# Hybrid decoder trunk on one core: where four chunks of the mixer's output are transposed, and how its early output products fill the slots of pairs 4 and 5

## The chip, the cores and the metric

One core of one Trainium2 chip runs the whole program. The time is the device time of one launch in microseconds; the median of the runs is compared. The engines are named as in the profile: PE is TensorE (products and transposes), PEld its weight loads, DVE is VectorE, ACT is ScalarE, POOL is GpSimd, SP is the engine that issues most DMAs.

## What is computed

Two layers, each a feed-forward block (SwiGLU, 2816 wide), a mixer and a second feed-forward block, every one followed by a layer norm of `alpha*x + block(x)`; 512 tokens, 1024 channels, float32. The change is within the mixer:

```
proj = x @ w_in                       # q, k, v of 6 forgetting heads, gates, q, k, v of 4 differential heads, SGU input
y_fox  = softmax(q k / 8 + c_q - c_k, causal) v            # 6 heads of 64 channels: chunks 0 to 2
a      = softmax(q1 k1) - lam * softmax(q2 k2)             # differential heads, two maps each
y_diff = rms_norm(a v) * g * (1 - lam_init)                # 4 heads of 64 channels: chunks 3 and 4
y_sgu  = u * (tril(w_s) @ layer_norm(g) + b_s)             # 6 heads of 64 channels: chunks 5 to 7
m = concat(y_fox, y_diff, y_sgu) @ w_out                   # 8 chunks of 128 channels
```

## The kernel before

Every float32 product is made from three products of split operands (high and low parts, written `hi` and `lo`): hi·hi, hi·lo, lo·hi (`product`, line 984). A split is a ScalarE copy for the high part and a VectorE or GpSimd subtraction for the low part. Weights come in tiles of 128 x 2048 in three slots, A, B and D; one tile in a slot is overwritten only when the products that read its predecessor are done.

**The head stage** (`heads`, line 1258) works on ten heads in five pairs, in the order forgetting, differential, forgetting, differential, forgetting. The code counts them 0 to 4 (`BODIES`); this text calls them pairs 1 to 5. A pair has 8 steps (`STEPS`): two heads times four blocks of 128 query rows, which attend to 128, 256, 384 and 512 keys. There are 40 steps, counted 0 to 39 (`G`); pair 4 is steps 24 to 31. In a step G, TensorE does in this order: `scores(G)`, one piece of other work ("slot 1"), `values(G - 2)`, `turn_p(G - 1)` (transposes of P), and another piece ("slot 2"). A differential head has two score maps. For each step VectorE takes the row maximum (L1872), ScalarE the exponential (L902) and the copy of the transposed P (L909, `p_out`), and VectorE divides and, for differential heads, mixes the two maps (L1887 to L1893). Each engine runs these in a fixed order, and waits on counting semaphores.

**The other work.** A generator `between` hands it out, one piece for each slot. In pairs 1 to 3 it is `project(l, b + 2)` (line 1194): the queries into PSUM bank 6, the keys into bank 7, 16 pieces of three 512-column products that read `xhi` and `xlo`, the mixer's input. The projection of pair 5 is the last reader of the input and of the projection's weight tiles in slot A. From pair 4 on it is `early(l)` (line 1233), for 32 slots in pairs 4 and 5:

- It waits for the key of pair 5 (`qk_ok`), then transposes the four chunks of `EARLY` (7, 0, 5, 6) of the mixer's output, one for each slot, into banks 6 and 7 (`turn_y`, line 1200; four transposes each). ScalarE copies them to `xhi` (`y_hi`, L916), and VectorE makes `xlo` (`y_lo`, L1833). The third and fourth turn wait for the low parts of the first and second.
- Then the early output products (`early_output`): for six of the eight output tiles the four early chunks, for the last two only two, 28 pieces. The first two chunks use the W_o tile in slot B, the other two the one in slot A. Tiles alternate between banks 6 and 7, and VectorE adds each finished one to the residual (`early_add`, L1513) at steps 28, 30, 32, 34, 36 and 38.

The W_o tile in slot A is split in halves: `query_half(5)` at step 20, `key_half(5)` at step 24 on ScalarE (L696), behind the exponentials, the copy of P and the key's eviction; GpSimd subtracts each half (L616). The second half waits until the last projection is done. `lo_ok["A"]` counts both. The remaining chunks (3, 1, 4, 2) are turned late (`LATE_TURNS`) and multiplied after the last step. `rms` does the differential norm on VectorE in pairs 3 and 5 (L1848 to L1864, `RMS_AT`). SP puts each pair's q and k to memory (L445) and refills slot A behind that; GpSimd loads them back as stacks for the scores.

The tiles `hl` (ten slots of 512 columns) and `thi` hold the split activations of the feed-forward blocks. In the head stage only slots 0 to 3 of `hl` are used, for q and k.

The lines that set the order of the early work:

```
EARLY = [(7, "B", 0), (0, "B", D), (5, "A", 0), (6, "A", D)]
...
                    next(between, None)
                    if G >= 2:
                        values(G - 2)
                    if G >= 1:
                        turn_p(G - 1)
                    next(between, None)
```

Of the kernel before, what the change touches and what calls it, by code (L numbers as in the profile page):

```python
# [5 lines left out]
ALU = mybir.AluOpType  # L6
# [80 lines left out]
EARLY_BODY = 3  # L87
WHOLE = 6
LATE_TURNS = {1: 4, 2: 5, STEPS - 1: 6}
LATE_BANK = [0, 2, 6, 7, 4, 5, 6, 7]  # L90
# [23 lines left out]
def build(nc, x_in, a_w, b_w, d_w, gb_row, gb_col, mix_row, mix_col, ws_in, lamv, out):  # L114
    ctx = ExitStack()
    with ctx:
# [215 lines left out]
        qhi, qlo, khi, klo = (hl[:, i, :] for i in range(4))  # L332
        pt = [s32[:, 1, :], s32[:, 3, :]]
        pos = res[64:65, 0, 0:S]
        mask = res[:, 1, 0:P]
# [13 lines left out]
        def stage(b):  # L349
            return stages[1 if b else 0]  # L350

        def is_diff(G):
# [330 lines left out]
        def _(act):  # L683
# [140 lines left out]
            for l in range(L):  # L824
# [86 lines left out]
                def y_hi(i):  # L911

                    act.wait_ge(yt_done, l * NC + i + 1)
                    c = (EARLY + LATE)[i][0]
                    b = 6 + i % 2 if i < len(EARLY) else 1 + 2 * (i % 2)
                    a.activation(xhi[:, c, :], bank[b][:, :], ACT.Copy).then_inc(ythi_ok, 1)  # L916

# [17 lines left out]
                for G in range(ALL):  # L935
                    b, k = divmod(G, STEPS)
                    exp(G)
                    if G:
                        p_out(G - 1)
                    if k == 0 and b + 1 < BODIES:  # L940
                        key(b + 1)
                        key_half(b + 2)
                    if k == NT and b < EARLY_BODY:
                        query(b + 2)
                        query_half(b + 3)
                    if b == EARLY_BODY and k < 2:
                        y_hi(2 * k)
                        y_hi(2 * k + 1)
                    if b == BODIES - 1:
                        if k in LATE_TURNS:  # L950
                            y_hi(LATE_TURNS[k])
                        if k in (NT, NT + 1):
                            act.wait_ge(s_done[0], count(l, ALL - STEPS + NT - 1, 0))
                            wo_half("D", l * D_ALL + D_WO, k - NT)
# [27 lines left out]
        def _(pe):  # L982
# [195 lines left out]
            def project(l, b):  # L1178

                n = l * A_ALL + A_QKS[b]  # L1180
                for g in range(2):
# [5 lines left out]
                    if b:  # L1187
                        pe.wait_ge(qk_ok, (l * BODIES + b - 1) * 2 + g + 1)
                    k = 0
                    for c in range(NC):  # L1190
# [9 lines left out]
            def turn_y(l, i):  # L1200

                c = (EARLY + LATE)[i][0]
                if i < len(EARLY):
                    b = 6 + i % 2
                else:
                    b = 1 + 2 * (i % 2)
                    if i < len(EARLY) + 2:
                        pe.wait_ge(mixp_ok, (l + 1) * DIFF_P * STEPS)
                if i % len(EARLY) >= 2:

                    pe.wait_ge(yt_ok, l * NC + i - 1)
# [8 lines left out]
            def early_output(l, u, n):  # L1220
# [3 lines left out]
                if n == 0 and u >= 2:  # L1224
                    pe.wait_ge(wo_free, l * 8 + u - 1)
                ins = product(bank[6 + u % 2][:, :], [(x(c, t * P, P), w(s, off + hf * 512, 512))],
                              start=(n == 0), stop=(n == len(EARLY) - 1))
# [5 lines left out]
            def early(l):  # L1233

                pe.wait_ge(qk_ok, (l + 1) * BODIES * 2 - 1)
                for i in range(len(EARLY)):
                    if i == 1:
                        pe.wait_ge(qk_ok, (l + 1) * BODIES * 2)
                    turn_y(l, i)
                    yield  # L1240
                pe.wait_ge(yt_ok, l * NC + len(EARLY))
                pe.wait_ge(lo_ok["B"], l * B_ALL + B_WO + 1 + AHEAD)
                for u in range(8):
                    for n in range(len(EARLY) if u < WHOLE else 2):
                        if n == 2:
                            pe.wait_ge(lo_ok["A"], l * A_ALL + A_WO + 1 + AHEAD)
                        early_output(l, u, n)
                        yield

            def heads(l):  # L1250
# [41 lines left out]
                for G in range(ALL):  # L1292
# [7 lines left out]
                    if G >= 1:  # L1300
                        turn_p(G - 1)
                    next(between, None)
                    if b == BODIES - 1 and k in LATE_TURNS:
                        turn_y(l, LATE_TURNS[k])
# [132 lines left out]
        def _(dve):  # L1437
# [329 lines left out]
            for l in range(L):  # L1767
# [60 lines left out]
                def y_lo(i):  # L1828

                    dve.wait_ge(ythi_ok, l * NC + i + 1)  # L1830
                    c = (EARLY + LATE)[i][0]
                    b = 6 + i % 2 if i < len(EARLY) else 1 + 2 * (i % 2)
                    v.tensor_tensor(xlo[:, c, :], bank[b][:, :], f32(xhi[:, c, :]), ALU.subtract).then_inc(yt_ok, 1)  # L1833

# [74 lines left out]
                for G in range(ALL):  # L1909
                    b, k = divmod(G, STEPS)  # L1910
                    adds = G - EARLY_BODY * STEPS - NT
                    if adds >= 0 and adds % 2 == 0 and adds // 2 < WHOLE:
                        early_add(adds // 2)
                    row_max(G)
# [8 lines left out]
                    if k == NT and b < EARLY_BODY:  # L1923
                        query(b + 2)
                    if b == EARLY_BODY and k < 2:
                        y_lo(2 * k)
                        y_lo(2 * k + 1)
                    if b == BODIES - 1 and k in LATE_TURNS:
# [99 lines left out]
```

## Time and profile before

| | |
|---|---|
| runs | 1914.09, 1914.52, 1915.98 us; median 1914.52 us |
| profiled execution | span 1915.8 us, first to last instruction |
| PE busy | 1879.1 us, 98% |
| DVE busy | 1414.4 us, 74% |
| ACT busy | 742.9 us, 39% |
| POOL busy | 216.9 us, 11% |
| mean granted TensorE clock | 0.993 |

The profile gives, for every engine, when each instruction began and how long it took, and in brackets how long the engine had been idle before it and which instruction's signal ended that. Nothing runs after the last instruction of the span. The granted clock is 1.00 at 2.4 GHz and 0.50 at 1.2 GHz. The head stage of layer 0 lies at about 461 to 580 us of the span, that of layer 1 at about 1408 to 1526 us.

### The profile page before, as it was taken

The page shows a single profiled execution, that of the slowest core. Times are in us where ns is not written, and L with a number is a line of the kernel's source. Part 1 is how long each engine was busy: PE and PEld are TensorE (multiplying, and loading weights), DVE is VectorE, ACT ScalarE, POOL GpSimd, SP SyncE. Part 2 cuts the span into 40 slices and gives each one's busy share as a digit, 9 for nine tenths or more (in the row PEclk, how much of TensorE's full clock was granted, in tenths as well). Part 3 has the DMA queues.
Part 4 walks back from the last instruction along what each step waited for, and adds up shares of the span by engine and source line. Part 5 has one row for each costly group of instructions (what it writes and reads, how often), then busy time and mean ns, then how long its engine had stood idle before and what let it go on. Part 6 is the DMA issues. An engine that isn't in the chain of part 4 may idle for free.

```text
span 1915.8 us, 25000 instructions
## 1 busy us (share of the span) xinstructions
PE 1879.1 (98%) x9121; PEld 1581.5 (83%) x9121; DVE 1414.4 (74%) x2059; ACT 742.9 (39%) x1114; POOL 216.9 (11%) x247
## 2 busy tenths in 40 slices
PE   7999999999999999999999999999999999999998
PEld 6888888888888888888888888888888888888887
DVE  7887877952666877787897877777536578777777
ACT  5333332435554524233254242333455443324243
POOL 2000000153314000000100000003343220000001
PEclk9999999999989999999999999999999999999999
DMA  5222223345732222222313222223557213222221
GB/s 219 93 109 88 109 88 132 108 131 169 209 89 89 110 88 109 88 109 88 132 68 130 88 109 88 109 110 108 176 139 217 66 67 121 113 95 109 88 110 44
DMA packets 43747, 215.95 MB, mean 113 GB/s; under 512 B 8756, under 2 KB 11252, under 8 KB 20008
## 3 DMA queue, kind: packets, MB, share of 16 engines
q1 hardware_dynamic: 40808, 199.30, 29.2%
q0 software_dynamic: 2880, 15.90, 3.6%
q8 instruction: 33, 0.54, 0.1%
q14 instruction: 26, 0.21, 0.0%
HBM read 197.23 MB, written 17.93 MB: 112 GB/s over the span
## 4 chain that ended last, share of the span: by engine, by line
PE 88%; DVE 5%; issue 2%; ACT 1%; DMA 1%; SPq 1%; POOL 1%; ACTq 0%; DVEq 0%; POOLq 0%
PE psum L992 80%; PE psum L1194 3%; PE psum L1288 1%; SPq L445 1%; DVE res L1513 1%; PE psum L1023 1%; DMA rawA<-in_a_w 1%; DVE st L1530 1%; PE psum L1278 1%; PE psum L1266 1%; DVE negm L1872 1%; DVE xlo L1469 0%; DMA gbc<-in_gb_col 0%; PE psum L1388 0%; ACT psum L902 0%
## 5 line engine op out<-in xcount | busy, mean ns | idle before, releaser
L992 PE MATMUL psum<-xhi,whiA 128*128 128x512 f32 (+1 forms) x768 | 287.4, 374 | 4.9 <-DVE xlo L1469 4.9
L992 PE MATMUL psum<-xlo,whiA 128*128 128x512 f32 (+1 forms) x768 | 285.9, 372 | 0.0
L992 PE MATMUL psum<-xhi,wloA 128*128 128x512 f32 (+1 forms) x768 | 285.8, 372 | 0.0
L992 PE MATMUL psum<-xhi,whiB 128*128 128x512 f32 x704 | 274.0, 389 | 0.0
L992 PE MATMUL psum<-xlo,whiB 128*128 128x512 f32 x704 | 273.9, 389 | 0.0
L992 PE MATMUL psum<-xhi,wloB 128*128 128x512 f32 x704 | 273.9, 389 | 0.0
L992 PE MATMUL psum<-whiD,hl 128*128 128x512 f32 x768 | 264.0, 390 | 1.9 <-DVE wloD L1446 1.9
L782 ACT ACTIVATE s<-psum 128x512 f32<-128x512 f32 x40 | 23.9, 598 | 540.7 <-PE psum L992 540.7
L1624 DVE SCALAR_TENSOR_TENSOR res<-psum,res 128x1024 f32<-128x1024 f32 x120 | 146.7, 1222 | 82.1 <-PE psum L992 82.1
L1624 DVE SCALAR_TENSOR_TENSOR nat<-psum,nat 128x1024 f32<-128x1024 f32 x144 | 175.8, 1221 | 26.4 <-PE psum L992 26.4
L992 PEld LDWEIGHTS psum<-xhi,whiA 128*128 128x128 f32 x768 | 145.4, 189 | 32.3 <-DVE xlo L1469 6.0
L992 PEld LDWEIGHTS psum<-whiD,hl 128*128 128x128 f32 x768 | 144.2, 188 | 32.6 <-issue 2.4
L992 PE MATMUL psum<-thi,hl 128*128 128x512 f32 x480 | 167.3, 389 | 0.0
L992 PEld LDWEIGHTS psum<-xlo,whiA 128*128 128x128 f32 x768 | 145.4, 189 | 25.0
L992 PEld LDWEIGHTS psum<-xhi,wloA 128*128 128x128 f32 x768 | 145.4, 189 | 25.0
L1446 DVE TENSOR_TENSOR wloA<-rawA,whiA 128x2048 fp32r<-128x2048 f32 x50 | 118.7, 2375 | 57.0 <-ACT whiA L689 57.0
L992 PEld LDWEIGHTS psum<-xhi,wloB 128*128 128x128 f32 x704 | 132.2, 188 | 27.6
L992 PEld LDWEIGHTS psum<-xlo,whiB 128*128 128x128 f32 x704 | 132.2, 188 | 27.3
L992 PEld LDWEIGHTS psum<-xhi,whiB 128*128 128x128 f32 x704 | 132.2, 188 | 27.2
L992 PE MATMUL psum<-wloD,hl 128*128 128x512 f32 x384 | 149.4, 389 | 0.0
L1446 DVE TENSOR_TENSOR wloB<-rawB,whiB 128x2048 fp32r<-128x2048 f32 x49 | 111.9, 2283 | 18.5 <-ACT whiB L689 18.5
L552 POOL TENSOR_TENSOR gbr<-gbr,alpha 128x1024 f32<-128x1024 f32 x6 | 11.2, 1896 | 937.4 <-DMA gbr<-in_gb_row 937.4
(217 smaller groups left out, 3543.1 us busy)
## 6 DMA issues: line engine op xcount, KB each, us to landing
rawA<-in_a_w SPq DMA_DIRECT2D x62, 1024.0 KB, 6.3
rawB<-in_b_w SPq DMA_DIRECT2D x54, 1024.0 KB, 4.7
rawD<-in_d_w SPq DMA_DIRECT2D x46, 1024.0 KB, 4.7
stacks<-hl SPq DMA_DIRECT2D x192, 64.0 KB, 1.7
whiD<-stacks POOLq DMA_DIRECT2D x10, 768.0 KB, 6.0
wloD<-stacks POOLq DMA_DIRECT2D x10, 768.0 KB, 5.9
gbr<-in_gb_row SPq DMA_DIRECT2D x6, 1024.0 KB, 8.5
stacks<-wloD SPq DMA_DIRECT2D x48, 64.0 KB, 1.7
```

The costliest lines, as they stand in the source:

```text
L445: sp.dma_start(stacks[b, s // 2, j * ROWS:(j + 1) * ROWS, tile + s % 2, :], part[s * ROWS:(s + 1) * ROWS, :].bitcast(F32)).then_inc(put_ok ...
L782: a.activation(silu["A"], bank[0][:, :], ACT.Silu).then_inc(silu_ok["A"], 1)
L992: ins = t_.matmul(out_, a_, b_, start=(start and k == 1), stop=(stop and k == n), skip_group_check=check)
L1023: ins = t_.transpose(bank[b][:, lo:lo + P], src[:, 2 * h + t, c * P:c * P + P], ident[:, :])
L1194: ins = t_.matmul(bank[6 + g][:, :], a_, b_, start=(k == 1), stop=(k == 3 * NC))
L1266: t_.matmul(bank[i][:, 0:n_], tile[0:STACK, n, t * P:t * P + P], tile[0:STACK, 2 + n, 0:n_], start=(n == 0 or maps == 2), stop=False)
L1278: ins = t_.transpose(bank[4 + G % 2][:, e * P:e * P + P], s32[:, 2 * (G % 2), e * P:e * P + P], ident[:, :])
L1288: ins = t_.matmul(bank[4 + G % 2][:, 0:HD], pt[G % 2][:, e * P:e * P + P], vals[:, e, vc:vc + HD], start=(e == 0), stop=(e == t))
L1446: v.tensor_tensor(wlo[s][:, :], raw[s][:, :], f32(whi[s][:, :]), ALU.subtract).then_inc(lo_ok[s], 1)
L1513: v.scalar_tensor_tensor(out=r, in0=bank[b][:, :], scalar=scale, in1=r, op0=ALU.mult, op1=ALU.add).then_inc(step, 1)
L1530: v.bn_stats(st[:, t, hf, :], res[:, t, hf * 512:hf * 512 + 512]).then_inc(st_ok, 1)
L1624: v.scalar_tensor_tensor(out=to, in0=psum[:, 4 + k % 2 * 2:6 + k % 2 * 2, :], scalar=0.5 * sign, in1=to, op0=ALU.mult, op1=ALU.add).then_i ...
```

## The change

The four early chunks are turned one by one in pairs 1 and 3: behind the second slot of steps 1, 5, 17 and 21, in the order of chunk 7 (bank 7), 5 (bank 6), 6 (bank 7) and 0 (bank 6). `TURNS` says so, as (pair counted from 0, step in the pair): (index in `EARLY`, bank). Since `xhi` and `xlo` are still read by the projections, the turned chunks go to other tiles: the high parts to slots 4 to 7 of `hl`, the low parts to slots 8 and 9 and to two thirds of `thi`. ScalarE and VectorE evict each in the step after. A turn waits until the last use of its bank is evicted, and a projection waits for the turned chunks that were in the banks before it.

`early` has no turns any more. Its 28 pieces go into the 32 slots of pairs 4 and 5 from the first on; every eighth slot (7, 15, 23 and 31) stays empty. The third piece, which is the first to use the W_o tile in slot A, thus moves from slot 6 (step 27) to slot 2 (step 25). The adds on VectorE move to steps 26, 29, 31, 33, 35 and 38.

```diff
+TURNS = {(0, 1): (0, 7), (0, 5): (2, 6), (2, 1): (3, 7), (2, 5): (1, 6)}
+TURN_AT = list(TURNS)
+EARLY_ITEMS = [(u, n) for u in range(8) for n in range(len(EARLY) if u < WHOLE else 2)]
+EARLY_SLOTS = [i for i in range(4 * STEPS) if i % 8 != 7]
+ADD_STEP = {EARLY_SLOTS[EARLY_ITEMS.index((u, len(EARLY) - 1))] // 2 + 1: u for u in range(WHOLE)}
...
+        yhi = [hl[:, 4 + i, :] for i in range(4)]
+        ylo = [hl[:, 8, :], hl[:, 9, :], thi[:, 0:S], thi[:, S:2 * S]]
...
+        def y_part(late, early, i):
+            if i < len(EARLY):
+                n, b = TURNS[TURN_AT[i]]
+                return early[n], b
+            return late[:, LATE[i - len(EARLY)][0], :], 1 + 2 * (i % 2)
...
@@ ScalarE: y_hi and its place
-                    a.activation(xhi[:, c, :], bank[b][:, :], ACT.Copy).then_inc(ythi_ok, 1)
+                    a.activation(to, bank[b][:, :], ACT.Copy).then_inc(ythi_ok, 1)
...
-                    if b == EARLY_BODY and k < 2:
-                        y_hi(2 * k)
-                        y_hi(2 * k + 1)
+                    if (b, k - 1) in TURNS:
+                        y_hi(TURN_AT.index((b, k - 1)))
...
@@ TensorE: project
+                    turned_before = sum(at < (b - 2, NT * g) for at in TURN_AT)
+                    if turned_before:
+                        pe.wait_ge(yt_ok, l * NC + turned_before)
...
@@ TensorE: turn_y
+                    at = TURN_AT[i]
+                    n, b = TURNS[at]
+                    c = EARLY[n][0]
+                    pe.wait_ge(qk_ok, (l * BODIES + at[0] + 1) * 2 + (3 if at[1] > NT else 2))
...
@@ TensorE: early
-                for i in range(len(EARLY)):
-                    if i == 1:
-                        pe.wait_ge(qk_ok, (l + 1) * BODIES * 2)
-                    turn_y(l, i)
-                    yield
                 pe.wait_ge(yt_ok, l * NC + len(EARLY))
                 pe.wait_ge(lo_ok["B"], l * B_ALL + B_WO + 1 + AHEAD)
-                for u in range(8):
-                    for n in range(len(EARLY) if u < WHOLE else 2):
+                for slot in range(4 * STEPS):
+                    if slot in EARLY_SLOTS:
+                        u, n = EARLY_ITEMS[EARLY_SLOTS.index(slot)]
                         if n == 2:
                             pe.wait_ge(lo_ok["A"], l * A_ALL + A_WO + 1 + AHEAD)
+                        if (u, n) == (1, 0):
+                            pe.wait_ge(qk_ok, (l + 1) * BODIES * 2)
                         early_output(l, u, n)
-                        yield
+                    yield
...
@@ TensorE: heads
+                    if (b, k) in TURNS:
+                        turn_y(l, TURN_AT.index((b, k)))
...
@@ VectorE
-                    adds = G - EARLY_BODY * STEPS - NT
-                    if adds >= 0 and adds % 2 == 0 and adds // 2 < WHOLE:
-                        early_add(adds // 2)
+                    if G - EARLY_BODY * STEPS in ADD_STEP:
+                        early_add(ADD_STEP[G - EARLY_BODY * STEPS])
...
-                    if b == EARLY_BODY and k < 2:
-                        y_lo(2 * k)
-                        y_lo(2 * k + 1)
+                    if (b, k - 1) in TURNS:
+                        y_lo(TURN_AT.index((b, k - 1)))
```

## Rows read from the trace of the kernel before

**Rows 1.** The page: busy time, share of the span and instructions of each engine
```profile
PE 1879.1 (98%) x9121; PEld 1581.5 (83%) x9121; DVE 1414.4 (74%) x2059; ACT 742.9 (39%) x1114; POOL 216.9 (11%) x247
```

**Rows 2.** Windows, as the first line names columns; stretches of head steps, start:end
```profile
core 0: us, PE busy (x) PEld busy (x) DVE busy (x) ACT busy (x) POOL busy (x), PEclk, DMA share, GB/s
481.43:492.32 10.89, 10.89 (x72) 9.76 (x70) 7.53 (x23) 6.14 (x19) 2.39 (x1) 1.00 0.72 164
526.58:544.15 17.57, 14.85 (x75) 13.15 (x74) 10.76 (x29) 10.30 (x28) 3.41 (x3) 0.71 0.55 153
1472.06:1489.65 17.59, 14.88 (x76) 13.16 (x74) 10.77 (x29) 10.08 (x27) 3.40 (x3) 0.71 0.59 162
531.95:542.10 10.15, 9.66 (x36) 8.59 (x37) 6.44 (x17) 4.00 (x12) 1.22 (x1) 0.50 0.57 173
475.62:478.73 3.11, 2.52 (x14) 1.91 (x13) 1.00 (x3) 2.63 (x7) 1.78 (x1) 1.00 0.73 171
520.72:523.88 3.16, 2.52 (x15) 1.91 (x13) 1.58 (x5) 2.63 (x7) 1.79 (x1) 1.00 1.10 265
1421.98:1424.74 2.76, 2.52 (x14) 1.91 (x13) 1.01 (x3) 2.47 (x7) 1.79 (x1) 1.00 0.98 243
1467.11:1469.36 2.25, 2.25 (x14) 1.99 (x13) 1.49 (x5) 1.72 (x7) 2.01 (x1) 1.00 1.02 232
```

**Rows 3.** Timeline of TensorE, start of pair 4, layer 0: start, us, line, work, [idle<-releaser]
```profile
528.05 0.61 PE L1278 MATMUL psum<-ident,s 128*128 128x128 f32 x4
530.56 0.66 PE L1217 MATMUL psum<-ident,nat 128*128 128x128 f32 x4 [1.90 <-DVE hl L1784]
...
537.19 0.79 PE L992 MATMUL psum<-whiB,xhi 128*128 128x512 f32 x1 [0.45 <-DVE xlo L1833]
```

**Rows 4.** Timeline of TensorE, layer 0, pair 5 and after: one turn, one item
```profile
561.40 0.60 PE L1217 MATMUL psum<-ident,nat 128*128 128x128 f32 x4
561.75 0.60 PE L1266 MATMUL psum<-whiD 97*128 97x384 f32 x2
...
582.22 0.40 PE L992 MATMUL psum<-whiA,xhi 128*128 128x512 f32 x1
...
582.92 0.39 PE L992 MATMUL psum<-whiD,xhi 128*128 128x512 f32 x1
```

**Rows 5.** Timeline of ScalarE and GpSimd, start of pair 4: the weight tile's chain
```profile
528.70 0.60 ACT L909 ACTIVATE s<-psum 128x512 f32<-128x512 f32 x1 [0.61 <-PE psum L1278]
...
529.67 1.06 ACT L696 ACTIVATE whiA<-rawA 128x1024 fp32r<-128x1024 f32 x1
...
530.80 2.36 POOL L616 TENSOR_TENSOR wloA<-rawA,whiA 128x1024 fp32r<-128x1024 f32 x1 [4.63 <-ACT whiA L696]
```

**Rows 6.** Timeline of TensorE, steps 8 and 9, pair 2, layer 0
```profile
483.19 0.61 PE L1278 MATMUL psum<-ident,s 128*128 128x128 f32 x4
...
484.73 0.44 PE L1194 MATMUL psum<-xhi,whiA 128*128 128x512 f32 x1
```

**Rows 7.** Timeline of TensorE, pairs 4 and 5, layer 0: waits for P's copy
```profile
556.50 0.88 PE L1288 MATMUL psum<-vals,s 128*128 128x64 f32 x6 [0.17 <-ACT s L909]
...
569.06 0.88 PE L1288 MATMUL psum<-vals,s 128*128 128x64 f32 x6 [0.64 <-ACT s L909]
```

**Rows 8.** Timeline, layer 0: evictions of a late turn, row maximum of step 19
```profile
562.03 0.60 ACT L916 ACTIVATE xhi<-psum 128x512 fp32r<-128x512 f32 x1 [0.87 <-PE psum L1217]
...
562.67 0.69 DVE L1833 TENSOR_TENSOR xlo<-psum,xhi 128x512 fp32r<-128x512 f32 x1 [1.61 <-ACT xhi L916]
...
513.25 0.69 DVE L1872 TENSOR_REDUCE negm<-psum 128x1 f32<-128x512 f32 x1 [0.57 <-PE psum L1268]
```

**Rows 9.** Timeline of GpSimd and VectorE, step 22 (layer 0) and in pair 5
```profile
522.09 2.37 POOL L616 TENSOR_TENSOR wloA<-rawA,whiA 128x1024 fp32r<-128x1024 f32 x1 [3.53 <-ACT whiA L696]
...
523.36 1.86 DVE L1864 TENSOR_TENSOR nat<-nat,mix 128x128 f32<-128x128 f32 x4
...
573.22 0.89 DVE L1864 TENSOR_TENSOR nat<-nat,mix 128x128 f32<-128x128 f32 x4
```

More of the change, by code:

```diff
@@ L913, in y_hi @@
                     act.wait_ge(yt_done, l * NC + i + 1)
-                    c = (EARLY + LATE)[i][0]
-                    b = 6 + i % 2 if i < len(EARLY) else 1 + 2 * (i % 2)
-                    a.activation(xhi[:, c, :], bank[b][:, :], ACT.Copy).then_inc(ythi_ok, 1)
+                    to, b = y_part(xhi, yhi, i)
+                    a.activation(to, bank[b][:, :], ACT.Copy).then_inc(ythi_ok, 1)
                 def wo_half(s, n, h):
@@ L1200, in turn_y @@
             def turn_y(l, i):
-                c = (EARLY + LATE)[i][0]
                 if i < len(EARLY):
-                    b = 6 + i % 2
+                    at = TURN_AT[i]
+                    n, b = TURNS[at]
+                    c = EARLY[n][0]
+                    pe.wait_ge(qk_ok, (l * BODIES + at[0] + 1) * 2 + (3 if at[1] > NT else 2))
                 else:
                     b = 1 + 2 * (i % 2)
+                    c = LATE[i - len(EARLY)][0]
                     if i < len(EARLY) + 2:
                         pe.wait_ge(mixp_ok, (l + 1) * DIFF_P * STEPS)
-                if i % len(EARLY) >= 2:
+                if i >= len(EARLY) + 2:
                     pe.wait_ge(yt_ok, l * NC + i - 1)
@@ L1225, in early_output @@
                     pe.wait_ge(wo_free, l * 8 + u - 1)
-                ins = product(bank[6 + u % 2][:, :], [(x(c, t * P, P), w(s, off + hf * 512, 512))],
+                ins = product(bank[6 + u % 2][:, :], [((yhi[n][:, t * P:t * P + P], ylo[n][:, t * P:t * P + P]), w(s, off + hf * 512, 512))],
                               start=(n == 0), stop=(n == len(EARLY) - 1))
@@ L1830, in y_lo @@
                     dve.wait_ge(ythi_ok, l * NC + i + 1)
-                    c = (EARLY + LATE)[i][0]
-                    b = 6 + i % 2 if i < len(EARLY) else 1 + 2 * (i % 2)
-                    v.tensor_tensor(xlo[:, c, :], bank[b][:, :], f32(xhi[:, c, :]), ALU.subtract).then_inc(yt_ok, 1)
+                    to, b = y_part(xlo, ylo, i)
+                    v.tensor_tensor(to, bank[b][:, :], f32(y_part(xhi, yhi, i)[0]), ALU.subtract).then_inc(yt_ok, 1)
                 def early_add(u):
```

## The prediction, made before the changed kernel ran

> **What bounds the kernel now.** I read the page first: the matrix engine is busy for 98% of the span, so any time between its products is time of the kernel [rows 1]. Then I cut the head stage of each layer into stretches [rows 2]. The first four steps of pair 2 take 10.89 us at a granted clock of 1.00, the first four of pair 4 (same widths, same two maps) take 17.57 us in layer 0 and 17.59 us in layer 1, at a mean clock of 0.71. They are the stretch that the change works on. The timeline of TensorE says why [rows 3]: after the transposes of P at 528.05 it waits 1.90 us for VectorE's low part of the key, later for low parts of turned chunks, 0.45 us the last time, and from 531.95 to 542.10 the clock is at 0.50, that is 1.2 instead of 2.4 GHz [rows 2]. Half of 10.15 us is 5.1 us lost to the clock, and the two waits shown are 2.35 us.
>
> **The change part by part.** Terms are for one layer, layer 0's times standing for both unless I say otherwise.
>
> *The four turns leave pair 4.* Pair 4 then fills its slots with early products from its first step. At full clock and without waits its first four steps would take what pair 2's take, 10.89 us, less one item, since slot 7 is left empty. An item is three products of 512 columns: from 582.22 to the next at 582.92, 0.70 us [rows 4]. So 10.19 us, a gain of 7.38 us if nothing else waits.
>
> *The third item waits for a weight tile.* Item 3 (n = 2) reads the W_o tile in slot A. That tile can't be split before the last product of pair 5's projection has read slot A, and the chain after it is long [rows 5]: ScalarE copies P of step 23 at 528.70, just after the transposes (528.05 + 0.61 = 528.66 [rows 3]), then the key, then from 529.67 the tile's second half, and GpSimd's subtraction runs from 530.80 for 2.36 us. The tile is ready at 533.16, 4.50 us after the transposes' end. Before, nobody asked for it until slot 6; now slot 2 does, in the second step. Where TensorE will be then is read from pair 2: its transposes start at 483.19 for 0.61 us, and the first product of the next step's first slot starts at 484.73 [rows 6], 0.93 us after their end. The wait is 4.50 - 0.93 = 3.57 us. Everything of step 25 behind the scores (values of step 23, transposes of 24) queues behind it on TensorE, and ScalarE and VectorE then wait for those.
>
> *The clock.* A wait of 1.90 us and little around it was enough for 1.2 GHz in both layers. With 3.57 us I expect it again. What it costs lies between 0 (no fall) and the 5.1 us of now. Before, 2.4 GHz came back 4.9 us after the last wait ended (537.19 to 542.10); half of that is 2.45 us. But busy stretches before 537.19 had not brought it back. I take 3.0 us, nearer to the first because no second wait follows. The four steps then take 10.19 + 3.57 + 3.0 = 16.8 us: a gain of only 0.8 us.
>
> *Slots 15, 23 and 31 are left empty too.* By the end of pair 5 the same 28 items are done, so 3 x 0.70 us of products are gone from the later steps. But slots 15 and 23 come in front of the values of steps 30 and 34, where TensorE already waits for ScalarE's copy of P, 0.17 and 0.64 us [rows 7]. There the 0.70 us turns into a longer wait. Slot 31 is free. Gain 0.7 us.
>
> *The moved VectorE adds* (steps 26, 29, 31, 33, 35, 38 instead of 28, 30, ... 38) I cost at nothing: the one that now stands in front of step 31's row maximum takes the place of the one in front of step 30's, in the same chain; likewise 35 for 34. If that cover is gone, one add is 0.68 us in front of a row maximum.
>
> *The four turns go to pairs 1 and 3.* Each is four transposes, 561.40 to 561.75, 0.35 us [rows 4]: 1.40 us in a layer. Two steps there are already longer than their work: with the work of step 22 of layer 1, 2.25 us, they take 3.11 and 3.16 us in layer 0 (pair 1 and pair 3), and 2.76 us in layer 1's pair 1 [rows 2], since ScalarE waits in front of a half split for a load whose start doesn't depend on TensorE's progress there. The two turns of a pair (0.70 us) come before or at that wait. So layer 0 pays 0, layer 1 pays 0.70 - 0.51 in pair 1 and 0.70 in pair 3, 0.89 us.
>
> *Their evictions* are 0.60 us of ScalarE and 0.69 us of VectorE each [rows 8]. They stand behind the copy of P and in front of the next row maximum. In steps 2, 6 and 18 VectorE is idle there (0.57 us in the tightest, step 18 [rows 8]), and the exponentials of one step are wanted only at the transposes of the next. Step 22 is full: the diff norm's last products start at 523.36 and the row maximum follows at once. In layer 0 those four products took 1.86 us, while in pair 5 they take 0.89 us at 573.22; they overlapped GpSimd's subtraction, 522.09 to 524.46 [rows 9]. With the eviction in front of them, some 0.4 us for the copy of P still ahead of it (an estimate, for 128x256 beside the 0.60 us of 128x512), then 0.60 and 0.69 us, they start near 525.1, after GpSimd is done, and end at 526.0 instead of 525.22: the row maximum is 0.8 us later, and with it (0.69 us) and an exponential of about that length still in time for the transposes at 528.05. So 0.
>
> The Trainium skill, "SBUF — State Buffer", section "Who interferes with whom", says that a VectorE instruction with two SBUF inputs is held while a GpSimd instruction reads SBUF, and not one with a single SBUF input. By that the products are indeed shorter once they start later; without it they would end near 527.0, and the whole chain to the weight tile would be about 0.7 us longer in layer 0, 1913.1 instead of 1912.4. The trace bears the rule out here, 1.86 against 0.89 us.
>
> *All waits added:* the projection of pairs 3 to 5 waits for the turned chunks' low parts; with an eviction some 1.3 us after the turn and two steps in between, 0. The new tiles belong to the feed-forward stage, which is over. No DMA is added.
>
> **Sum.** Layer 0: -0.8 - 0.7 = -1.5 us. Layer 1: -0.8 - 0.7 + 0.9 = -0.6 us. Together -2.1 us. The profiled execution's span is 1915.8 us, 1.3 us above the median of the runs; I take the difference to the median: 1914.5 - 2.1 = 1912.4 us. A measurement of this kernel can tell about 0.2%, 3.8 us, from no change: below 1910.7 is faster, above 1918.3 slower.
>
> **Rivals.**
> - *Wait without a fall of the clock.* The wait of 3.57 us stands alone between two dense stretches; the one of now had turns and short products around it. Then each layer gains 3.0 us more, but the copy of P that step 28 waits for shows instead, about 1 us: 2 x 2.0 = 4.0 us, 1908.4 us. Against it: 1.90 us was enough. The Trainium skill, "TensorE: Matmul & The Clock Gate", section "Why this matters for your kernels", asks for no idle gaps between bursts of products, or the clock halves; it speaks against this change's new gap. Chance 0.16.
> - *The gap closes as described,* the weight tile being no wait: both layers gain 7.38 + 0.70, less the 1 us at step 28, less 0.9 in layer 1: 13.3 us, 1901.2 us. The chain of rows 5 speaks against it. Chance 0.04.
> - *Slower: the evictions get in the way.* The place is VectorE in pairs 1 and 3, the low part in front of the row maximum. Price if nothing hides: 0.60 + 0.69 = 1.29 us for each of eight turns, 10.3 us, 1922.7 us. It decides once more than 5.9 of the 10.3 us show, which is more than half of the eight turns; the idle time above speaks against it in three of four. Chance 0.15.
> - The forecast, a trade of one wait for another: 0.65.
>
> **How the numbers follow.** Faster: 0.16 + 0.04 and 0.01 of the forecast's own spread, 0.21. Slower 0.15. Same 0.64. With the clock at either bound in both layers the forecast runs from 1908.4 to 1912.4 + 2 x 2.1 = 1916.6 us. The range takes in the first rival, an error of 1 us below it, and part of the third: 1907.5 to 1918.5 us.
>
> **What would show it.** Right: in pair 4's second step, one idle time of 3 to 4.5 us in front of a product of whiA, released by GpSimd's wloA, in both layers; no wait for the key's low part; a granted clock of 0.50 starting within the wait or soon after it for 5 to 8 us; the first four steps of pair 4 at 16 to 18 us; waits of 0.7 to 1.4 us in front of the values of steps 30 and 34; pairs 1 and 3 longer by 0 to 0.9 us. Wrong: a wait under 2 us there, a clock of 1.00 throughout, or pairs 1 and 3 longer by more than 2 us with row maxima late behind the evictions.

## The result, and the profile after

The changed kernel took 1918.40 us (median of 15 runs, 1915.11 to 1920.60), the kernel before beside it 1914.54 us (15 runs, 1912.79 to 1917.82). The ratio is 1.0016, interval 1.0010 to 1.0022: some 3.1 us slower, under 0.2%, but on the other side from the forecast of 1912.4 us. One execution of the kernel before, in the later run `again`, took 3171.74 us at a mean granted clock of 0.59 and is left out.

The page of the profile after, its span and the busy times of the engines (before: [rows 1]):

```profile
span 1916.7 us, 25000 instructions
PE 1873.7 (98%) x9121; PEld 1575.4 (82%) x9121; DVE 1412.3 (74%) x2059; ACT 741.0 (39%) x1114; POOL 215.7 (11%) x247
```

TensorE is busy for 5.4 us less and the span is 0.9 us longer, so TensorE stands idle for 6.3 us more. Note also how span and time differ: this execution took 1918.4 us for a span of 1916.7, and every execution of both kernels showed 1.7 to 1.8 us between the two. The span of 1915.8 us of before thus belongs to an execution of about 1917.5 us. I come back to this.

The head stage in windows. Columns as in [rows 2]. First the kernel after: steps 0 to 23, then steps 24 to 31, of layer 0 and of layer 1; then steps 31 and 32 of layer 0, and two low stretches of the clock.

```profile
462.21:528.50 66.29, 65.09 (x404) 56.23 (x402) 37.69 (x113) 36.63 (x101) 26.96 (x22) 1.00 0.74 201
528.50:554.62 26.12, 22.58 (x135) 19.63 (x134) 16.07 (x48) 12.37 (x40) 4.05 (x5) 0.93 0.51 132
1408.09:1473.61 65.52, 64.81 (x404) 56.48 (x403) 37.50 (x113) 36.75 (x101) 27.06 (x22) 1.00 0.74 203
1473.61:1500.95 27.34, 23.41 (x136) 20.37 (x134) 16.16 (x48) 12.38 (x40) 4.06 (x5) 0.88 0.48 133
552.59:559.49 6.90, 5.38 (x34) 4.42 (x33) 4.62 (x12) 3.45 (x11) 0.99 (x2) 1.00 0.52 115
536.90:540.31 3.41, 3.41 (x13) 3.02 (x13) 2.35 (x7) 0.33 (x2) 0.00 (x0) 0.51 0.68 137
1478.20:1485.80 7.60, 5.27 (x18) 4.70 (x19) 1.92 (x6) 1.30 (x5) 2.28 (x1) 0.55 0.56 141
```

The same stretches of the profiled execution of before that the prediction used:

```profile
461.58:526.58 65.00, 63.37 (x388) 54.68 (x386) 36.34 (x109) 35.50 (x99) 27.07 (x22) 1.00 0.78 205
526.58:555.13 28.55, 25.83 (x145) 22.98 (x144) 19.30 (x53) 14.97 (x44) 4.41 (x5) 0.82 0.46 122
1407.94:1472.06 64.12, 63.31 (x387) 54.83 (x386) 36.14 (x109) 35.72 (x99) 27.07 (x22) 1.00 0.76 206
1472.06:1500.63 28.57, 25.86 (x146) 22.99 (x144) 19.29 (x53) 14.77 (x43) 4.40 (x5) 0.82 0.48 128
552.22:558.68 6.46, 6.18 (x38) 5.06 (x36) 4.62 (x12) 3.06 (x11) 1.00 (x2) 1.00 0.51 115
```

Pairs 1 to 3 grew by 1.29 and 1.40 us, the eight steps of pair 4 shrank by 2.43 and 1.23 us, and steps 31 and 32 together grew by 0.44 us. So in these two executions the change wins time in pair 4 and hands it back on both sides.

The start of pair 4 in layer 0, all engines (start, us, engine, line, work, idle before it and its releaser; only the rows of the chain, other instructions between them are left out), and the same wait in layer 1; it answers to [rows 3] and [rows 5]:

```profile
530.28 0.61 PE L1296 MATMUL psum<-ident,s 128*128 128x128 f32 x4
530.92 0.60 ACT L925 ACTIVATE s<-psum 128x512 f32<-128x512 f32 x1 [0.72 <-PE psum L1296]
531.42 0.59 ACT L857 ACTIVATE hl<-psum 128x512 fp32r<-128x512 f32 x1
531.90 1.06 ACT L712 ACTIVATE whiA<-rawA 128x1024 fp32r<-128x1024 f32 x1
533.03 2.34 POOL L632 TENSOR_TENSOR wloA<-rawA,whiA 128x1024 fp32r<-128x1024 f32 x1 [4.95 <-ACT whiA L712]
535.42 0.50 PE L1006 MATMUL psum<-whiA,hl 128*128 128x512 f32 x1 [3.43 <-POOL wloA L632]
...
1480.53 0.80 PE L1006 MATMUL psum<-whiA,hl 128*128 128x512 f32 x1 [3.44 <-POOL wloA L632]
```

This is the forecast's chain, link by link: transposes of P, copy of P, key, second half of the weight tile, subtraction, and TensorE idle for 3.43 us in front of a product of whiA. The clock falls to 0.50 behind it, at 536.85 in layer 0 (in the other profile of this kernel, `after_again`, already inside the wait). The waits of before for the key and for low parts are gone. Later, TensorE waits for the copy of P in front of the values of steps 30 and 34, which answers to [rows 7]:

```profile
557.32 0.88 PE L1306 MATMUL psum<-vals,s 128*128 128x64 f32 x6 [1.41 <-ACT s L925]
569.89 0.88 PE L1306 MATMUL psum<-vals,s 128*128 128x64 f32 x6 [1.37 <-ACT s L925]
```

### The profile page after: what moved, and what is told of

Read it like the earlier page. It is cut to its first block, busy times and chain, and to the rows that moved or that the text cites. A ratio compares the mean times of both kernels' runs of the same rounds, so it can differ in the third digit from the quotient of the medians.

```text
span 1916.7 us, 25000 instructions
## 1 busy us (share of the span) xinstructions
PE 1873.7 (98%) x9121; PEld 1575.4 (82%) x9121; DVE 1412.3 (74%) x2059; ACT 741.0 (39%) x1114; POOL 215.7 (11%) x247
## 4 chain that ended last, share of the span: by engine, by line
PE 87%; DVE 5%; issue 2%; ACT 2%; DMA 1%; SPq 1%; POOL 1%; ACTq 0%; DVEq 0%; POOLq 0%
PE psum L1006 79%; PE psum L1211 4%; PE psum L1306 1%; DVE res L1533 1%; SPq L461 1%; DMA rawA<-in_a_w 1%; PE psum L1037 1%; DVE st L1550 1%; PE psum L1296 1%; DVE negm L1891 1%; PE psum L1284 1%; DVE xlo L1489 0%; ACT psum L918 0%; DMA gbc<-in_gb_col 0%; PE psum L1408 0%
```

## The experiments

Each kernel is the changed one with the edit shown, unless it says otherwise. Ratios are to the kernel before on the same chip. Three theories were tested, the first two from the start. *Weight tile* (W in the expectations): the early demand for the second half of the tile, and the low clock after it, eat what pair 4 gains. *Turns* (E): the turns in pairs 1 and 3, and the empty slots, cost more than forecast, and the rest is small. *Clock* (C): the fall behind the wait, not the wait itself, is the larger loss. The expectations of the runs state again what each theory gives there.

**again: the kernel before, profiled once more.** No edit.

> The kernel before, unchanged, for a second profile. Theory A (the clock's share of pair 4 differs from execution to execution, and the profile before happened to show the longest): the low clock of layer 0 and layer 1 in the first steps of pair 4 lasts about 3.4 or 6.8 us here in at least one layer, instead of 10.2 us in both, and the span is 1 to 4 us below 1915.8. Rival (the low clock always lasts 10.2 us): both layers again 10.2 us, first four steps 17.6 us, span 1915.8 within 1 us.

1914.79 us, ratio 0.9996 (0.9986 to 1.0005). Its head stage in windows, steps 0 to 23 and 24 to 31 of each layer:

```profile
462.03:526.05 64.02, 63.13 (x387) 54.69 (x386) 36.23 (x109) 35.52 (x99) 27.12 (x22) 1.00 0.78 208
526.05:552.51 26.46, 22.86 (x145) 20.45 (x144) 19.20 (x53) 14.48 (x44) 4.41 (x5) 0.94 0.52 135
1405.32:1469.42 64.10, 63.16 (x388) 54.80 (x386) 35.72 (x109) 36.11 (x99) 27.09 (x22) 1.00 0.77 209
1469.42:1498.01 28.59, 25.88 (x145) 22.86 (x144) 19.29 (x53) 14.58 (x42) 4.39 (x5) 0.82 0.49 127
```

Layer 1 is as before. Layer 0 is 0.98 us shorter in pairs 1 to 3 and 2.09 us shorter in pair 4: the clock is at 0.50 for 3.4 us there, not 10.2. Theory A holds. Most executions of the same kernel lie within some 3 us of its median, and the one that I had reckoned from was a long one.

**again2 and after_again: a third profile of before, a second of after.** No edits.

> The kernel before, a third profile. Theory A: low clock of 3.4, 6.8 or 10.2 us in each layer, 10.2 us in both being the rare case; span between 1911 and 1916 us, the higher the longer the low clock.

> The changed kernel, unchanged, for a second profile and beside the kernel before on the same chip. Waits as in its first profile: 3.4 us for the weight tile and 1.4 us twice in front of values, in both layers; the low clock in pairs 4 and 5 anywhere from 3.4 to 10.2 us in each layer; ratio to the kernel before 1.001 to 1.002.

again2 took 1914.91 us, low clock again 3.4 us in layer 0 and 10.2 us in layer 1. after_again took 1917.28 us, ratio 1.0012 (1.0003 to 1.0021), low clock 6.8 us in both layers, where the first profile had 3.4 and 6.8. Over three profiles of before and two of after, a layer's head stage up to the turn of chunk 2 is:

| us in a layer, mean | steps 0 to 23 | 24 to 31 | 32 to the last turn | sum |
|---|---|---|---|---|
| before | 64.28 | 27.90 | 32.82 | 125.00 |
| after | 65.47 | 27.03 | 33.49 | 125.98 |

0.98 us in each layer is 2.0 us in all, of 3.1 that the runs show. These five executions are not the typical ones: their spans have a mean of 1914.0 before and 1915.6 after, 1.6 us apart, while the medians of all executions with a span on record (73 and 26) are 1913.0 and 1916.1.

**order: products of the slot-B tile first.** The third and fourth item trade places with the first two of the next output tile, so the tile in slot A is wanted two slots later.

```diff
+EARLY_ITEMS[0:8] = [(0, 0), (0, 1), (1, 0), (1, 1), (0, 2), (0, 3), (1, 2), (1, 3)]
```

> The changed kernel with pieces (1,0) and (1,1), which need only the W_o tile in slot B, ahead of (0,2) and (0,3). Theory W (the wait for the weight tile in slot A and the low clock behind it eat the gain): the 3.4 us wait in step 25 goes; 0.7 us for the key of pair 5 may take its place at slot 2 and up to 0.5 us for the tile at slot 4; the clock stays at 1.00; 7 to 12 us below the changed kernel, ratio to the kernel before 0.995 to 0.998. Rival E (turns in pairs 1 and 3 and empty slots are what costs): within 2 us of the changed kernel, ratio 1.0005 to 1.002.

1909.83 us, ratio 0.9983 (0.9973 to 0.9993). By the medians that is 8.0 us less than the change as made (1917.8 us over its 26 executions), by the ratios some 6 us; the ratio is at the edge of the 0.995 to 0.998 that I expected. Windows of steps 24 to 31 in both layers:

```profile
526.69:549.46 22.77, 21.02 (x136) 18.28 (x134) 15.97 (x48) 12.36 (x40) 4.10 (x5) 1.00 0.59 154
1468.77:1491.78 23.01, 21.02 (x136) 18.27 (x134) 15.97 (x48) 12.38 (x40) 4.10 (x5) 1.00 0.61 162
```

In the timeline of TensorE, the wait that is left in the first four steps of layer 0:

```profile
530.98 0.50 PE L1007 MATMUL psum<-whiB,hl 128*128 128x512 f32 x1 [0.79 <-DVE hl L1805]
```

The wait for the tile is gone, one of 0.79 us for the key's low part is in its place (the item of the next output tile needs bank 7), and the clock stays at 1.00. The two windows are 3.35 and 4.33 us shorter than in the first profile of the kernel after, 7.7 us together: the gain is here. That shows the weight tile theory's mechanism, and that it was the largest loss in the new kernel.

**late4: only the turns moved.** Slots 0 to 3 stay empty, and every item and add stands where it stood before.

```diff
-EARLY_SLOTS = [i for i in range(4 * STEPS) if i % 8 != 7]
+EARLY_SLOTS = list(range(4, 32))
```

> The changed kernel with the pieces in slots 4 to 31 as in the kernel before, slots 0 to 3 empty, adds at the old steps: only the turns are moved. Theory W: no wait for the weight tile; TensorE has nothing to fill steps 24 and 25 and waits there for the exponential and P's copy, some 3 us, and the clock falls in one layer or none; the first four steps of pair 4 take 12 to 14 us; 2 to 6 us below the changed kernel, ratio 0.998 to 1.000. Rival E: the turns cost the same as in the changed kernel, ratio 1.001 to 1.002.

1907.65 us, ratio 0.9961 (0.9948 to 0.9975): 10 us below the changed kernel, where I had expected 2 to 6. The windows of steps 24 to 31 in both layers:

```profile
526.59:549.52 22.93, 20.80 (x129) 17.45 (x128) 16.59 (x50) 12.74 (x41) 4.40 (x5) 1.00 0.62 158
1467.32:1490.61 23.29, 20.82 (x129) 17.46 (x128) 16.60 (x50) 12.75 (x41) 4.39 (x5) 1.00 0.62 163
```

Timeline, TensorE's waits in the first seven microseconds of pair 4, layer 0:

```profile
527.74 0.85 PE L1306 MATMUL psum<-vals,s 128*128 128x64 f32 x6 [0.59 <-ACT s L925]
529.72 1.10 PE L1306 MATMUL psum<-vals,s 128*128 128x64 f32 x8 [0.27 <-ACT s L925]
532.48 0.44 PE L1306 MATMUL psum<-vals,s 128*128 128x64 f32 x2 [0.26 <-ACT s L925]
533.41 0.44 PE L1296 MATMUL psum<-ident,s 128*128 128x128 f32 x2 [0.50 <-DVE s L1912]
```

Four short waits, 1.6 us together where I had expected 3, and no fall of the clock, in layer 1 not even behind one of 0.85 us (at 1474.49). The first four steps take 10.86 and 11.22 us, not 12 to 14; they hold four items here and seven in the changed kernel. Moving the turns alone is worth about 7 us; refilling the slots that they leave, as the change does it, makes the kernel 10 us slower again (1917.8 against 1907.65). The turns theory falls as an explanation of the result: all four turns are in this kernel. What the turns do cost is worked out below.

**slots: the empty slots at the end.** The 28 items run through slots 0 to 27.

```diff
-EARLY_SLOTS = [i for i in range(4 * STEPS) if i % 8 != 7]
+EARLY_SLOTS = list(range(28))
```

> The changed kernel with the 28 pieces in slots 0 to 27 and slots 28 to 31 empty. Theory W: the wait for the weight tile stays at 3.4 us; the waits in front of the values of steps 30 and 34 fall from 1.4 to 0.2 and 0.7 us since slots 15 and 23 are filled, and the empty slots stand where TensorE waits for nothing: 1.4 us less in a layer, 3 us in all, ratio 1.000 to the kernel before. Rival E (empty slots are the main cost): 5 us or more, ratio 0.998 or less. If the waits only move behind the new empty slots: no change, 1.0016.

1914.71 us, ratio 0.9998 (0.9989 to 1.0007), 3.1 us below the change. In layer 0's view of waits (line, waited for: us in all, times, longest) the tile's stays, and those for the copy of P shrink from 3.8 us to 1.6 us:

```profile
PE psum L1006 <- POOL wloA L632: 3.4, 1, 3.4
PE psum L1306 <- ACT s L925: 1.6, 4, 0.6
```

In front of the values of steps 30 and 34 they fall from 1.41 and 1.37 us to 0.18 and 0.63, 2.0 us together and as expected. (Of the 3.8 us, 0.8 are waits in pairs 1 and 3, where the two kernels are alike; of the 1.6 us, 0.65 is a new wait at 574.45.) So the empty slots 15 and 23, in front of waits for P, bought nothing. Part of the 3.1 us may be the clock's, which was at 0.50 for 3.4 us in both layers here, less than in three of the four head stages profiled of the change as made; how much is open.

**adds: one VectorE add moved behind the row maximum of step 31.**

```diff
+ADD_STEP = {2: 0, 5: 1, 8: 2, 9: 3, 11: 4, 14: 5}
```

> The changed kernel with the third add behind step 31's row maximum, in front of step 32's. Theory: the add in front of step 31's row maximum is in the chain that the values of step 30 wait for; their wait falls from 1.4 to about 0.9 us in both layers, steps 31 and 32 together from 6.9 to 6.4 us. My prediction's premise (it takes the place of another add in the same chain, cost nothing): the wait stays at 1.4 us.

One execution, 1914.93 us. VectorE at step 31 in the kernel after (the mix of two maps, the add, the row maxima), then the same place with the add moved, and the wait that follows there:

```profile
553.59 0.62 DVE L1912 SCALAR_TENSOR_TENSOR s<-psum,wlam,s 128x384 f32<-128x384 f32 x1
554.12 0.68 DVE L1533 SCALAR_TENSOR_TENSOR res<-psum,res 128x512 f32<-128x512 f32 x1
554.72 1.28 DVE L1891 TENSOR_REDUCE negm<-psum 128x1 f32<-128x512 f32 x2
```

```profile
552.12 0.62 DVE L1912 SCALAR_TENSOR_TENSOR s<-psum,wlam,s 128x384 f32<-128x384 f32 x1
552.66 1.28 DVE L1891 TENSOR_REDUCE negm<-psum 128x1 f32<-128x512 f32 x2
555.25 0.88 PE L1306 MATMUL psum<-vals,s 128*128 128x64 f32 x6 [0.82 <-ACT s L925]
```

And the window of steps 31 and 32 there:

```profile
551.12:557.43 6.31, 5.39 (x34) 4.42 (x33) 4.61 (x12) 2.92 (x11) 0.99 (x2) 1.00 0.54 121
```

The wait in front of step 30's values falls from 1.41 to 0.82 us, steps 31 and 32 from 6.90 to 6.31 us, in layer 1 from 6.91 to 6.31 us. 0.82 is the 0.17 of before plus most of the 0.70 us of the empty slot, as forecast; the other 0.6 us was the add. The total of one execution is too coarse for 1.2 us.

**both: order and slots together.**

```diff
+EARLY_ITEMS[0:8] = [(0, 0), (0, 1), (1, 0), (1, 1), (0, 2), (0, 3), (1, 2), (1, 3)]
+EARLY_SLOTS = list(range(28))
```

> The order of the experiment before (slot B's pieces of two output tiles first) and the 28 pieces in slots 0 to 27. If each does what it did alone: no wait for the weight tile, clock 1.00, waits of 0.2 and 0.6 us in front of the values of steps 30 and 34 instead of 1.4 and 1.4: 2.5 to 3.5 us below the order alone, 1906 to 1907.5 us, ratio 0.996 to 0.997. If the slots only help where the clock is low: 1909 to 1910 us.

1906.26 us (6 runs, 1904.60 to 1907.73), ratio 0.9953 (0.9941 to 0.9965). Steps 24 to 31:

```profile
527.69:551.77 24.08, 22.72 (x142) 19.47 (x141) 17.27 (x51) 12.86 (x41) 4.41 (x5) 1.00 0.56 149
1467.65:1491.98 24.33, 22.74 (x142) 19.48 (x140) 17.29 (x51) 12.88 (x41) 4.41 (x5) 1.00 0.59 157
```

The windows are longer than those of `order`, since no slot is empty in them, and the later steps win more than that: 120.2 us for the head stage of each layer, against 121.2 and 122.3. By the medians the gains add up: 8.0 and 3.1 us apart, 11.5 together. It beats the kernel before and the one after. It does not beat `late4` beyond the noise (1906.26 against 1907.65 us, overlapping intervals): most of the gain is the moved turns', and the refilling of slots 0 to 3 in its best order adds little.

**gap: order, with slots 2 and 3 left empty,** so that no item waits for the key.

```diff
+EARLY_ITEMS[0:8] = [(0, 0), (0, 1), (1, 0), (1, 1), (0, 2), (0, 3), (1, 2), (1, 3)]
+EARLY_SLOTS = [0, 1] + list(range(4, 30))
```

> The same order, with slots 2, 3, 30 and 31 empty, so that neither the key of pair 5 nor the weight tile is waited for. Theory: the 0.8 us wait for the key at slot 2 goes, but TensorE has two pieces less in step 25, where the chain of row maximum, exponential and P's copy then sets the pace, as it does in steps 24 and 25 of the kernel with the turns alone moved: within 1 us of the kernel with both edits, clock 1.00, 1906 to 1908 us.

1906.75 us (5 runs), ratio 0.9957 (0.9944 to 0.9970), the same as `both` within the intervals. Once no wait of several microseconds was left, it mattered little here where two empty slots stand.

**fill: twelve products in the wait.** Their result is read by nobody; they keep TensorE at work while the tile is split.

```diff
                         if n == 2:
+                            if (u, n) == (0, 2):
+                                pe.wait_ge(qk_ok, (l + 1) * BODIES * 2)
+                                for _ in range(12):
+                                    t_.matmul(bank[7][:, :], yhi[0][:, 0:P], whi["B"][:, 0:512], start=True, stop=True)
                             pe.wait_ge(lo_ok["A"], l * A_ALL + A_WO + 1 + AHEAD)
```

> The changed kernel with twelve extra products of 512 columns into bank 7 in front of the wait for the weight tile (their result is used nowhere; bank 7's first piece starts afresh). They need the key of pair 5 evicted, about 0.7 us, and run 2.8 us, so they fill the wait and don't shorten it. Theory C (behind the wait, the low clock costs a few us more in each execution): the tile's product starts within 0.5 us of where it starts in the changed kernel, the clock stays at 1.00 in both layers, 3 to 5 us below the changed kernel, ratio to the kernel before 0.999 to 1.000. Rival (the clock costs nothing much, since waits of ScalarE's chain would show in its place): ratio 1.001 to 1.002, with the waits in front of the values of steps 26 to 34 longer by what the clock gave back.

1917.33 us, ratio 1.0014 (1.0005 to 1.0023): no gain, though steps 24 to 31 are shorter and at full clock. The added products in the timeline:

```profile
531.74 3.01 PE L1264 MATMUL psum<-whiB,hl 128*128 128x512 f32 x12 [0.78 <-DVE hl L1808]
```

Windows of layer 0: steps 24 to 31, then from step 32 up to 570.00, then the low stretch in it:

```profile
527.47:552.97 25.50, 23.84 (x147) 20.59 (x146) 15.85 (x48) 12.35 (x40) 4.11 (x5) 1.00 0.51 136
552.97:570.00 17.03, 14.15 (x82) 11.86 (x81) 9.53 (x26) 7.25 (x21) 0.80 (x3) 0.90 0.21 48
556.50:560.00 3.50, 3.40 (x13) 2.97 (x13) 1.40 (x5) 1.05 (x3) 0.00 (x0) 0.51 0.21 42
```

The clock did not fall at the tile. It fell later, behind the wait of 1.41 us for the copy of P at 555.66, in both layers. The first four steps of pair 4 take 13.96 us in layer 0 and 14.21 us in layer 1, against 15.34 to 16.55 in the kernel after, though the products hold the tile's first product up by 0.2 us. This gain of 2.0 us in the mean is lost again further on: a wait of 0.77 us in front of the values of step 26 (543.58), and steps 31 and 32 at 7.90 us instead of 6.90, at the low clock. The clock theory's time, 3 to 5 us below the changed kernel, and its clock of 1.00 throughout did not come; the rival's ratio did, and its waits in part. Why the clock fell there, and not in `order` behind a wait of the same 1.41 us (552.15 in its timeline), is open.

**fillslots: fill and slots together,** so that the later waits for P are short as well. Beside the four lines of `fill`:

```diff
-EARLY_SLOTS = [i for i in range(4 * STEPS) if i % 8 != 7]
+EARLY_SLOTS = list(range(28))
```

> The twelve extra products in front of the wait for the weight tile, and the 28 pieces in slots 0 to 27. In the experiment with the extra products alone the clock held through the wait and fell later, behind the 1.4 us waits that the empty slots 15 and 23 leave. Theory: with those slots filled it doesn't fall at all; the products fill the wait, so the difference to the kernel with slots 0 to 27 alone (3.4 us of low clock in each layer when profiled) is what the low clock costs there: 1 to 2 us in a layer, less what shows as waits for P's copy instead: 1911 to 1913 us. Rival (the low clock's cost is all hidden behind the chain): 1914 to 1915 us, as without the products.

1911.64 us (9 runs), ratio 0.9979 (0.9969 to 0.9989). First four steps of pair 4 in both layers; then those of `slots`, which differs by the twelve products alone:

```profile
528.05:542.80 14.75, 13.96 (x84) 12.05 (x82) 8.01 (x25) 7.05 (x21) 3.43 (x3) 1.00 0.61 159
1470.77:1485.77 15.00, 14.08 (x84) 12.05 (x83) 8.12 (x25) 7.07 (x21) 3.43 (x3) 1.00 0.69 187
```

```profile
526.60:542.72 16.12, 12.69 (x72) 11.05 (x70) 8.49 (x25) 8.20 (x25) 3.38 (x3) 0.89 0.65 173
1469.62:1485.76 16.14, 12.70 (x71) 11.17 (x70) 8.41 (x25) 7.27 (x23) 3.38 (x3) 0.89 0.68 181
```

The clock stays at 1.00 in both head stages, and these four steps are 1.37 and 1.14 us shorter. The time is in the expected 1911 to 1913 us, 3.1 us below `slots` by the medians. But that is not the price of the low clock in the head stages. Here they are whole, from step 0 to the turn of chunk 2, of `slots` and then of `fillslots`, layer 0 and layer 1:

```profile
461.63:584.62 122.99, 117.60 (x723) 102.29 (x722) 70.84 (x210) 65.05 (x177) 41.55 (x33) 0.99 0.56 152
1404.64:1528.51 123.87, 118.07 (x723) 102.36 (x722) 70.82 (x210) 65.09 (x177) 41.64 (x33) 0.99 0.57 152
```

```profile
463.05:585.74 122.69, 119.46 (x736) 103.18 (x735) 70.65 (x210) 64.89 (x177) 41.58 (x33) 1.00 0.56 152
1405.78:1528.73 122.95, 119.60 (x735) 103.22 (x734) 70.73 (x210) 65.00 (x177) 41.70 (x33) 1.00 0.57 152
```

They are 0.3 and 0.9 us shorter, 1.2 us together: for a stretch of 3.4 us at 0.50, 1.1 to 1.4 us show in the four steps themselves, and steps 28 to 31 give 1.0 and 0.2 us of it back. The other 1.9 us of the medians lie outside the head stages or in what one profiled execution differs from the typical one. The mean granted clock of all executions points at the first: its median is 0.996 for `slots` and 0.999 for `fillslots`, and two stretches of 3.4 us at 0.50 make only 0.002 of that.

## Why the prediction was wrong

The miss is 6.0 us: 1918.4 against 1912.4. Set against the two profiled executions, it comes from two places of about equal size, and not from the main mechanism.

**The baseline, 3.0 us.** This step failed: "The profiled execution's span is 1915.8 us, 1.3 us above the median of the runs". It compared a span with times of executions, which lie 1.7 us higher. Like with like, the execution took about 1917.5 us, 3.0 above the median of 1914.5. Its excess over `again` is seen row by row, 0.98 us in pairs 1 to 3 and 2.09 us in pair 4, both in layer 0. I subtracted gains measured on a long execution from a typical time. On its own time, 1917.5 - 2.1, the forecast would have been 1915.4 us, and the time lost to the clock would have been put at 4.0 us in a layer (a mean of 8.0 us at 0.50 over the three profiles), not 5.1.

**The steps, 3.0 us.** Against the same profiled execution, layer 0 and layer 1:

| stretch | forecast | measured |
|---|---|---|
| steps 0 to 23 | 0, +0.9 | +1.29, +1.40 |
| steps 24 to 30 | -0.8, -0.8 | -1.55, -0.35 |
| steps 31 and 32 | 0, 0 | +0.44, +0.46 |
| step 33 to the last turn | -0.7, -0.7 | -0.67, -0.67 |
| sum of both layers | -2.1 | +0.35 |

The remaining 0.5 us (the spans differ by 0.85) lie outside the head stages: that of layer 0 starts 0.63 us later, at 462.21 instead of 461.58, behind 3.4 us at a clock of 0.50 from 41.92 on that the profile of before hasn't got there. `again` has it too, at 41.77, so it is not the change's.

- *Pairs 1 to 3:* "So layer 0 pays 0" failed, and 0.35 us for each turn was too little. The waits that were to hide the turns are not in every execution. Pairs 1 and 3 by themselves, in three profiles of before (in the order `before`, `again`, `again2`) and three of kernels with the turns (`after`, `after_again`, `late4`, alike up to step 23):

| us | pair 1, layer 0 | pair 1, layer 1 | pair 3, layer 0 | pair 3, layer 1 |
|---|---|---|---|---|
| before | 19.85, 19.02, 19.10 | 19.50, 19.77, 20.10 | 22.58, 22.43, 22.45 | 21.67, 21.67, 21.67 |
| with the turns | 20.42, 19.88, 19.88 | 19.88, 19.87, 19.88 | 23.29, 22.51, 22.54 | 22.54, 22.51, 22.57 |

  Where no wait hides them (pair 3 of layer 1) two turns cost 0.84 us or more, 0.42 each. Where there is one (pair 3 of layer 0) they cost some 0.1 us at most in two of the three profiles: the hiding works. But in pair 1 of layer 0 the wait that the forecast counted on stood in one of three profiles of before, the long one that I had read, 0.59 us; without it that pair pays 0.8 us too. Over all ten profiles of kernels with the turns, steps 0 to 23 take 65.17 us in the mean against 64.28: 0.89 us in each layer, 1.8 in all, where 0.9 was forecast. The +1.29 of layer 0 in the table is more than that, since the first profile of the kernel after was long there.
- *Evictions:* right. The low part in front of step 22's row maximum takes 0.69 us at 526.22, and the norm's products behind it 0.89 us at 526.83 instead of the 1.86 us of [rows 9]. The Trainium skill, "SBUF — State Buffer", section "Who interferes with whom", says that two SBUF inputs are held by a GpSimd read; the trace agrees, 0.89 us once GpSimd is done. The slower rival is this mechanism, and it did not happen, though the time came out on its side.
- *The weight tile:* right, 3.43 and 3.44 us against 3.57, by the chain named, and the experiment `order` shows that it decides.
- *The clock:* the fall was right, its price too high. It fell in both layers, for 3.4 to 6.8 us, mean 6.0 over two profiles, against 5 to 8 forecast. The first four steps took 15.34, 16.17, 16.55 and 16.34 us over the two profiles, against 16.8. Beside the 13.96 and 14.21 us of `fill`, which has full clock there, the low clock cost 2.0 us in the mean, where 3.0 were taken. The spread of single stretches is what made -0.8 come out as -1.55 and -0.35. The rival without a fall fell. The Trainium skill, "TensorE: Matmul & The Clock Gate", section "Why this matters for your kernels", warns of idle gaps between bursts of products, or the clock halves; the trace agrees for the gap of 3.43 us. A gap alone does not settle it: the clock fell behind 1.41 us in `fill` and stayed up behind 1.41 us in `order`.
- *The moved adds:* "I cost at nothing" failed for step 31. The add stands in front of the maxima that release the copy of P for step 30's values; where it had stood, the waits behind it were short. By `adds` it costs 0.6 us in a layer; the cover gone, the price that the text named was 0.68.
- *Slots 15, 23 and 31:* right. Waits of 1.41 and 1.37 us (0.87 and 1.34 foreseen, the rest of the first being the add), and -0.67 us for slot 31.

Nothing in the prediction asked whether the items were worth moving at all. `late4` answers it: with the items where they were, the first four steps take 10.86 and 11.22 us, with three more of them in front 15.34 to 16.55, though three items are only 2.1 us of products.

## What to carry to other kernels

Before a product is moved ahead, find for each of its operands when that operand is ready, and move first those that are ready: here swapping four items by two slots turned 3 us of loss into 3 to 5 us of gain. But ask first what the moving is worth: leaving the four slots empty gave 1907.65 us, filling them in the best order 1906.26. Empty slots belong where no wait stands behind them, and a wait on the bottleneck engine costs its own length and at times a fall of the clock after it. A wait that is to hide new work must be there in every execution, not in the one that was profiled. Reckon a change from several profiled executions, and set each span against its own execution's time before a median is brought in.

## What the runs showed of the hardware that was not expected

- The low clock of one unchanged kernel varies from one execution to the next: 10.2 or 3.4 us in layer 0 of the kernel before, 3.4 or 6.8 us in layer 0 of the one after, with the same first wait in front, 1.90 us before and 3.43 after. In the 62 executions of before that ran beside the experiments, the 6 at a mean granted clock of 0.993 took spans of 1915.6 us on average, the 19 at 0.996 1912.5 and the 3 at 0.998 1910.9. One execution can thus not price it.
- Waits of 0.3 to 0.6 us, four in six microseconds (`late4`), left the clock at 1.00, and so did those of 0.79, 0.85 and 1.41 us in `order`; in `fill` it fell behind one of 1.41 us.
- Filling an idle stretch with unused products kept the clock up there. Alone it gained nothing, and the clock fell at a later wait. With the later waits short too, the head stages were 1.2 us shorter in the profile and the medians 3.1 us.
